# The landing buffer of a mixture-of-experts stage: its loads issued from GpSimd's own queue instead of SyncE's

## The chip, the cores and the metric

One core of a Trainium2 chip runs the whole program. The metric is the device time of one execution in microseconds. The program is one launch that computes two transformer blocks; the change touches one stage of the first of them, the experts.

## The reference, cut to what matters

Both blocks work on 512 tokens of width 1024, in float32. The stage in question is the feed-forward part of the first block: each token is sent to 4 of 32 experts, and the rows of an expert are gathered and padded to whole blocks.

```python
logits = (xt @ w_router) + b_router
top_v, top_e = lax.top_k(logits, 4)            # 512 tokens x 4 of 32 experts
top_w = softmax(top_v)
# rows sorted by expert, padded per expert to whole blocks; then for each block of rows, expert e:
g = xb @ w_gate[e] + b_gate[e]                 # 1024 x 1024, the first product
u = xb @ w_up[e] + b_up[e]                     # 1024 x 1024, the second
g = minimum(g, 7); u = clip(u, -7, 7)
act = (u + 1) * (g * sigmoid(1.702 * g))
y = act @ w_down[e] + b_down[e]                # 1024 x 1024, the third
```

## The kernel before, in words

The kernel pads an expert's rows to blocks of 64 (the reference to 128; the outcome is the same). An expert's weights are three matrices of 4 MB, each cut into 4 units of 1 MB that lie in memory as 128 rows of 8 KB: units 0 to 3 are the gate matrix, 4 to 7 the up matrix, 8 to 11 the down matrix. In on-chip memory there is one place for each of the 12 units, `wt[:, 0..11]`, and a landing buffer `land[:, 0..3]` for the 4 units of the third product (down) alone. So at most 16 units are held at once, while the stage moves 31 x 12 of them (expert 0's are loaded by the stage before).

TensorE (`pe`) walks over the blocks. For block i it runs gate(i), two transposes, up(i), and then down(i - 1): the third product is one block late. Each unit is 8 matmuls of 512 columns (two halves of the array work side by side). After a unit it raises `s_mm[u]`. Before a unit it waits: for units 0 to 7 on `s_w[u]` (the load has landed), for units 8 to 11 on `s_cp[u - 8]` (GpSimd has copied it out of the landing buffer).

SyncE (`sp`) loops over the experts e = 1 to 31 and issues all loads of an expert in a fixed order: gate units 0 to 3, the biases (`biases(e)`, line 1111), up units 4 to 7 (all through `unit(u)`, line 1122), and then the four landing units (line 1133). `done` is the number of the last block of expert e - 1. Each gate or up unit waits until TensorE has used that place for the last block of the expert before; each landing unit waits until GpSimd has emptied that row, `s_cp[u]` at least e.

GpSimd (`pool`) loops over the same experts: for each of the 4 landing rows it waits for the load, and for TensorE to have finished with the place in `wt` (`s_mm[8 + u]`), and then copies the row over (line 1150). That wait ends while TensorE runs the third product of the last block of expert e - 1, which comes behind gate and up of expert e's first block.

ScalarE issues the loads of the blocks' rows (`load`, line 1231, two of 128 KB a block) and the stores of the results (`store`, line 1235, two of 128 KB a block) in a hardware queue of its own, q10. SyncE's loads go in the hardware queue q1. What GpSimd issues goes in the software queue q0. All queues are served by the same 16 DMA engines.

Of the kernel before, what the change touches and what calls it, by code (L numbers as in the profile page):

```python
# [33 lines left out]
NE, TOPK = 32, 4  # L34
# [16 lines left out]
def take(nc, name):  # L51

    TAKEN.append(nc.alloc_semaphore(name))
    return TAKEN[-1]
# [9 lines left out]
def build(nc, A, K, out, dram):  # L64

    with ExitStack() as ctx:
# [11 lines left out]
        with ExitStack() as early:  # L78
            wt = sb("wt", [P, NUNIT, 2, D], c=early)
            s_w = [nc.alloc_semaphore(f"e_w{u}") for u in range(NUNIT)]  # L80
            with ExitStack() as first:
                flat = wt[:, :, :, :].rearrange("p u k n -> p (u k n)")
                qkv = flat[:, 0:12 * D].rearrange("p (b a t w) -> p b a t w", b=2, a=3, t=NT)
                ring = flat[:, 12 * D:].rearrange("p (n k w) -> p n k w", n=3, k=KD)
                gB = flat[:, 0:KD * T].rearrange("p (f t) -> p f t", f=KD)
                mT = flat[:, 6 * D:6 * D + KD * T].rearrange("p (f t) -> p f t", f=KD)
                yT = sb("yT", [P, 2, NT, T], c=first)
                hT = sb("hT", [P, KD, T], c=first)
                s_wb = [nc.alloc_semaphore(f"g_wb{u}") for u in range(2)]
                first_mix(nc, A, K, dram, ident, tri, mod, x, ps, yT, hT, qkv, ring, mT, gB, s_wb)  # L90
                end_stage(nc)
                first_merge(nc, A, K, dram, ident, tri, mod, x, ps, yT, hT, ring, mT, gB, blocks, pos, w4, wt, s_w, s_wb)
                end_stage(nc)
            experts(nc, A, K, dram, ident, ps, blocks, wt, s_w)
            end_stage(nc)
# [979 lines left out]
def experts(nc, A, K, dram, ident, ps, blocks, wt, s_w):  # L1075

    with ExitStack() as ctx:
        def sb(name, shape, dt=F32):
            return ctx.enter_context(nc.sbuf_tensor("e_" + name, shape, dt))

        def sem(name):
            return take(nc, "e_" + name)
# [10 lines left out]
        land = sb("land", [P, 4, 2, D])  # L1093
# [2 lines left out]
        TAKEN.extend(s_w)  # L1096
        s_mm = [sem(f"mm{u}") for u in range(NUNIT)]
        s_cp = [sem(f"cp{u}") for u in range(4)]
        s_raw, s_shuf, s_xg = (sem(n) for n in ("raw", "shuf", "xg"))
        s_xt, s_xT, s_g, s_sig, s_act = (sem(n) for n in ("xt", "xT", "g", "sig", "act"))  # L1100
        s_at, s_aT, s_y, s_out, s_dve, s_go = (sem(n) for n in ("at", "aTs", "y", "out", "dve", "go"))
# [4 lines left out]
        with nc.Block() as block:  # L1106
            @block.sync
            def _(sp):
                def biases(e):
                    for q in range(4):  # L1110
                        sp.dma_start(raw[32 * q:32 * q + 1, :, :].rearrange("p a n -> p (a n)"),
                                     A["b_exp"][bass.ds(e, 1)].rearrange("e q n -> e (q n)")[:, q * 3 * W:(q + 1) * 3 * W]
                                     ).then_inc(s_raw, 16)

                sp.wait_ge(s_shuf, 1)
                biases(0)
                with sp.Fori(1, NE) as e:
                    done = sp.value_load(blocks[0:1, bass.ds(e + FIRST, 1)], min_val=0, max_val=NBLK)

                    def unit(u):  # L1120
                        sp.wait_ge(s_mm[u], done * 2 + 2)
                        sp.dma_start(wt[:, u].rearrange("p k n -> p (k n)"),
                                     A["w_exp"][bass.ds(e, 1)].rearrange("e u p n -> p (e u) n")[:, u, :]).then_inc(s_w[u], 16)

                    for u in range(4):
                        unit(u)
                    sp.wait_ge(s_shuf, done + 1)
                    biases(e)
                    for u in range(4, 8):
                        unit(u)  # L1130
                    for u in range(4):
                        sp.wait_ge(s_cp[u], e)
                        sp.dma_start(land[:, u].rearrange("p k n -> p (k n)"),
                                     A["w_exp"][bass.ds(e, 1)].rearrange("e u p n -> p (e u) n")[:, 8 + u, :]).then_inc(s_w[8 + u], 16)
                for u in range(NUNIT):
                    sp.wait_ge(s_w[u], 16 * NE)
                sp.wait_ge(s_raw, 64 * NE)

            @block.gpsimd
            def _(pool):  # L1140
                for u in range(4):
                    pool.wait_ge(s_w[8 + u], 16)
                    pool.sem_inc(s_cp[u], 1)
                with pool.Fori(1, NE) as e:
                    done = pool.value_load(blocks[0:1, bass.ds(e + FIRST, 1)], min_val=0, max_val=NBLK)
                    for u in range(4):
                        pool.wait_ge(s_w[8 + u], e * 16 + 16)
                        pool.wait_ge(s_mm[8 + u], done * 2 + 2)
                        pool.sem_inc(s_go, 1)
                        nc.gpsimd.tensor_copy(wt[:, 8 + u], land[:, u]).then_inc(s_cp[u], 1)  # L1150
                for u in range(4):
                    pool.wait_ge(s_cp[u], NE)

# [1661 lines left out]
```

## Time and profile before

| | us |
|---|---|
| median of 3 runs | 3922.02 |
| lowest, highest run | 3916.95, 3926.28 |
| the profiled execution's own time | 3920.97 |
| its span | 3919.2 |

The page of the profile has a first part with the busy time of each engine, a second with the span in 40 slices of 98 us (busy tenths of each engine, the granted clock of TensorE, the share in which the DMA engines were busy, and GB/s), a list of the queues, and a list of the costliest groups of instructions. The stage of the experts is some 1255 us of the span, from about 799 to about 2054 us, slices 9 to 21. Timelines give for one engine the start, the time taken, the instruction, and in brackets how long the engine had been idle just before and what ended that.

### The profile page before, as it was taken

The page shows a single profiled execution, that of the slowest core. Times are in us where ns is not written, and L with a number is a line of the kernel's source. Part 1 is how long each engine was busy: PE and PEld are TensorE (multiplying, and loading weights), DVE is VectorE, ACT ScalarE, POOL GpSimd, SP SyncE. Part 2 cuts the span into 40 slices and gives each one's busy share as a digit, 9 for nine tenths or more (in the row PEclk, how much of TensorE's full clock was granted, in tenths as well). Part 3 has the DMA queues.
Part 4 walks back from the last instruction along what each step waited for, and adds up shares of the span by engine and source line. Part 5 has one row for each costly group of instructions (what it writes and reads, how often), then busy time and mean ns, then how long its engine had stood idle before and what let it go on. Part 6 is the DMA issues. An engine that isn't in the chain of part 4 may idle for free. (4 is left out here: it accounts for less than half of the span.)

```text
span 3919.2 us, 37507 instructions
## 1 busy us (share of the span) xinstructions
PE 3376.9 (86%) x11902; PEld 1491.6 (38%) x11903; DVE 1928.6 (49%) x3951; ACT 688.9 (18%) x1609; POOL 964.2 (25%) x829
## 2 busy tenths in 40 slices
PE   7997999788889987999887987898878888788887
PEld 3345454422223322333224456544333333333332
DVE  5834323622333322333225226486666766766776
ACT  1011121000000000000002125422222222222212
POOL 1000000112221222012122013134443444444443
PEclk8998999789999999999998998999998999999998
DMA  9834434469999999197976201179999999999998
GB/s 330 285 124 166 152 122 157 187 240 411 370 375 353 363 407 374 62 380 270 397 290 242 81 6 44 44 291 378 421 421 399 417 417 412 421 404 421 415 422 341
DMA packets 194149, 1157.36 MB, mean 295 GB/s; under 512 B 25659, under 2 KB 27995, under 8 KB 74356
## 3 DMA queue, kind: packets, MB, share of 16 engines
q1 hardware_dynamic: 97140, 565.17, 37.3%
q0 software_dynamic: 80576, 564.05, 35.2%
q10 hardware_dynamic: 16320, 26.75, 2.2%
q8 instruction: 57, 0.93, 0.1%
q14 instruction: 56, 0.46, 0.0%
HBM read 1128.96 MB, written 48.68 MB: 300 GB/s over the span
## 5 line engine op out<-in xcount | busy, mean ns | idle before, releaser
L1170 PE MATMUL ps<-wt,e_xT 128*64 128x512 f32 x3200 | 743.4, 609 | 114.2 <-DMA wt<-in_w_exp 113.0
L2628 DVE SCALAR_TENSOR_TENSOR mod<-uv,mix 128x1024 f32<-128x1024 f32 x512 | 626.9, 1225 | 352.4 <-DMA uv<-in_peer_uv,q_picks 347.7
L2312 POOL DMA_INDIRECT uv<-in_peer_uv,q_picks x512 | 575.4, 1124 | 773.4 <-PE ps L2403 702.7
L2403 PE MATMUL ps<-uv,q_dg 128*128 128x512 f32 x1024 | 519.9, 664 | 134.4 <-ACT q_dg L2480 129.9
L2403 PE MATMUL ps<-uv,tri 128*128 128x512 f32 x1024 | 472.2, 615 | 75.9 <-ACT tri L2480 75.9
L1150 POOL COPY wt<-e_land 128x2048 f32<-128x2048 f32 x124 | 248.0, 2030 | 1004.3 <-PE ps L1170 951.8
L1170 PEld LDWEIGHTS ps<-wt,e_xT 128*64 128x64 f32 x3200 | 219.7, 139 | 596.2 <-issue 380.8
L2403 PEld LDWEIGHTS ps<-uv,q_dg 128*128 128x128 f32 x1024 | 213.7, 214 | 431.7 <-issue 431.7
L1170 PE MATMUL ps<-wt,e_aT 128*64 128x512 f32 x1600 | 354.2, 595 | 2.8 <-ACT e_aT L1223 2.8
L2403 PEld LDWEIGHTS ps<-uv,tri 128*128 128x128 f32 x1024 | 197.8, 197 | 345.6 <-issue 345.6
L472 PE MATMUL ps<-hT,wt 128*128 128x512 f32 x640 | 285.1, 602 | 1.5 <-DVE wt L799 1.5
L1289 DVE TENSOR_TENSOR e_ut<-ps,e_bias 128x512 f32<-128x512 f32 x50 | 34.6, 692 | 400.6 <-PE ps L1170 400.6
L1223 ACT COPY e_aT<-ps 128x512 f32<-128x512 f32 x50 | 29.3, 585 | 1095.0 <-PE ps L1158 1072.5
L1170 PEld LDWEIGHTS ps<-wt,e_aT 128*64 128x64 f32 x1600 | 115.3, 138 | 232.8 <-issue 232.8
L2474 ACT ACTIVATE q_ap<-q_ap 128x4 f32<-128x4 f32 (+1 forms) x131 | 26.9, 205 | 893.6 <-DVE mod L2628 893.6
L472 PEld LDWEIGHTS ps<-hT,wt 128*128 128x128 f32 x640 | 120.8, 192 | 151.0 <-issue 145.1
L684 DVE SCALAR_TENSOR_TENSOR x<-mod,small,x 128x512 f32<-128x512 f32 x168 | 129.3, 769 | 32.5 <-DMA mod<-in_w_ada_units 20.9
L1306 DVE TENSOR_TENSOR e_yb<-ps,e_bias 128x512 f32<-128x512 f32 x50 | 34.6, 692 | 171.9 <-PE ps L1170 171.9
L472 PE MATMUL ps<-wt,hT 128*128 128x512 f32 x256 | 116.5, 611 | 0.7 <-ACT hT L574 0.7
L1278 DVE LOAD_MASK_SELECT e_bias<-e_raw x50 | 0.7, 14 | 211.0 <-DMA e_raw<-in_b_exp 163.8
L2358 PE MATMUL ps<-q_hT,q_wq 128*128 128x512 f32 x224 | 98.4, 592 | 0.0
L405 POOL COPY mod<-hT 128x1024 f32<-128x1024 f32 x4 | 8.2, 2063 | 365.5 <-PE ps L472 365.5
(458 smaller groups left out, 3508.3 us busy)
## 6 DMA issues: line engine op xcount, KB each, us to landing
wt<-in_w_exp SPq DMA_DIRECT2D x260, 1024.0 KB, 20.0
e_land<-in_w_exp SPq DMA_DIRECT2D x124, 1024.0 KB, 24.2
wt<-in_w_in_units SPq DMA_DIRECT2D x15, 2048.0 KB, 11.2
mod<-in_w_mod_units SPq DMA_DIRECT2D x48, 512.0 KB
scratch_xs<-const_zeros SPq DMA_DIRECT2D x8, 2080.0 KB
mod<-in_w_ada_units SPq DMA_DIRECT2D x32, 512.0 KB
p_ring<-in_w_in SPq DMA_DIRECT2D x7, 2048.0 KB, 10.6
e_xg<-scratch_xs ACTq DMA_DIRECT2D x104, 128.0 KB
```

The costliest lines, as they stand in the source:

```text
L472: last = nc.tensor.matmul(ps[:, j, :], lhs, rhs, start=(k == 0), stop=(k == kt - 1))
L684: last = dve.scalar_tensor_tensor(at, quarter[:, q, kk, :], cs[:, v, k:k + 1], at, ALU.mult, ALU.add)
L1150: nc.gpsimd.tensor_copy(wt[:, 8 + u], land[:, u]).then_inc(s_cp[u], 1)
L1170: ins = nc.tensor.matmul(ps[64 * h:64 * h + 64, at, :], lhs[:, k % 4, 64 * (k // 4):64 * (k // 4) + 64], wt[:, u, a, h * W:(h + 1) * W], s ...
L1223: nc.scalar.copy(dst, ps[:, at, :].rearrange("p (k q) -> p k q", k=4)).then_inc(kept, 1)
L1289: link(dve.tensor_tensor(ut[:, :], ps[:, U, :], bias[:, 1, :], ALU.add))
L1306: dve.tensor_tensor(yb[:, :], ps[:, Y, :], bias[:, 3, :], ALU.add).then_inc(s_y, 1)
L2312: pool.indirect_dma_start(out=uv[:, slot(n), :, :].rearrange("p a d -> p (a d)"), out_offset=None, in_=A["peer_uv"], in_offset=bass.Indire ...
L2358: last = nc.tensor.matmul(ps[:, 6 + c, :], wq[:, h % 2, k, c * NK:(c + 1) * NK], hT[:, k, :], start=(k == 0), stop=(k == KD - 1))
L2403: last = nc.tensor.matmul(acc(t)[:, c, :], dg(n), uv[:, slot(n), 1, c * W:(c + 1) * W], start=fresh, stop=closing)
L2474: act.activation(at, at, ACT.Gelu).then_inc(s_ge, 1)
L2628: dve.scalar_tensor_tensor(junk[:, n % 2, :], uv[:, slot(n), 0, :], 1.0, mix[:, tile_of(k), :], ALU.mult, ALU.mult, accum_out=ap[:, k % 2, ...
```

## The change

The four landing loads leave SyncE's loop and are issued by GpSimd. Expert 1's are issued at the start of the stage, when expert 0's third-product units have landed in `wt`; expert e + 1's unit u is issued right after the copy of expert e's unit u has ended, before the next copy. A new semaphore for each row, `s_ld[u]`, counts their landing. The loop over experts on GpSimd is split so that the last expert has no load behind it.

```diff
+        s_ld = [sem(f"ld{u}") for u in range(4)]
@@ sync
                     for u in range(4, 8):
                         unit(u)
-                    for u in range(4):
-                        sp.wait_ge(s_cp[u], e)
-                        sp.dma_start(land[:, u].rearrange("p k n -> p (k n)"),
-                                     A["w_exp"][bass.ds(e, 1)].rearrange("e u p n -> p (e u) n")[:, 8 + u, :]).then_inc(s_w[8 + u], 16)
                 for u in range(NUNIT):
-                    sp.wait_ge(s_w[u], 16 * NE)
+                    sp.wait_ge(s_w[u], 16 * NE if u < 8 else 16)
@@ gpsimd
                 for u in range(4):
                     pool.wait_ge(s_w[8 + u], 16)
                     pool.sem_inc(s_cp[u], 1)
-                with pool.Fori(1, NE) as e:
+                    pool.dma_start(land[:, u].rearrange("p k n -> p (k n)"), A["w_exp"][1, 8 + u]).then_inc(s_ld[u], 16)
+
+                def unload(e, following):
                     done = pool.value_load(blocks[0:1, bass.ds(e + FIRST, 1)], min_val=0, max_val=NBLK)
                     for u in range(4):
-                        pool.wait_ge(s_w[8 + u], e * 16 + 16)
+                        pool.wait_ge(s_ld[u], e * 16)
                         pool.wait_ge(s_mm[8 + u], done * 2 + 2)
                         pool.sem_inc(s_go, 1)
                         nc.gpsimd.tensor_copy(wt[:, 8 + u], land[:, u]).then_inc(s_cp[u], 1)
+                        if following:
+                            pool.wait_ge(s_cp[u], e + 1)
+                            pool.dma_start(land[:, u].rearrange("p k n -> p (k n)"),
+                                           A["w_exp"][bass.ds(e + 1, 1)].rearrange("e u p n -> p (e u) n")[:, 8 + u, :]).then_inc(s_ld[u], 16)
+
+                with pool.Fori(1, NE - 1) as e:
+                    unload(e, True)
+                unload(NE - 1, False)
```

## Rows read from the trace of the kernel before

**Rows 1.** The page, 40 slices: share of DMA in tenths; slices 9 to 21 are the stage.

```profile
DMA  9834434469999999197976201179999999999998
```

**Rows 2.** Waits, 780 to 2160 us: who waited for whom, us in total, times, longest.

```profile
SPq L1122 <- PE ps L1170: 657.5, 185, 112.0
...
PE ps L1170 <- DMA wt<-in_w_exp: 113.0, 106, 3.6
```

**Rows 3.** Timeline of GpSimd: copies out of the landing buffer, and three DMA issues.

```profile
994.34 6.06 POOL L1150 COPY wt<-e_land 128x2048 f32<-128x2048 f32 x3 [25.00 <-PE ps L1170]
1027.48 8.09 POOL L1150 COPY wt<-e_land 128x2048 f32<-128x2048 f32 x4 [25.02 <-PE ps L1170]
1071.03 8.09 POOL L1150 COPY wt<-e_land 128x2048 f32<-128x2048 f32 x4 [35.46 <-PE ps L1170]
1099.15 1.93 POOL L1150 COPY wt<-e_land 128x2048 f32<-128x2048 f32 x1 [20.03 <-PE ps L1170]
...
1559.75 8.08 POOL L1150 COPY wt<-e_land 128x2048 f32<-128x2048 f32 x4 [24.83 <-PE ps L1170]
1690.39 8.09 POOL L1150 COPY wt<-e_land 128x2048 f32<-128x2048 f32 x4 [122.56 <-PE ps L1170]
...
2068.91 2.81 POOL L1414 DMA_DIRECT2D p_cw<-in_conv_w  x3
```

**Rows 4.** Timeline of SyncE's queue from the load of expert 7's gate units on.

```profile
1034.35 5.48 SPq L1122 DMA_DIRECT2D wt<-in_w_exp  x4
...
1048.05 1.88 SPq L1133 DMA_DIRECT2D e_land<-in_w_exp  x4
...
1106.02 5.48 SPq L1122 DMA_DIRECT2D wt<-in_w_exp  x4
```

**Rows 5.** Timeline of TensorE over experts 6 (two blocks), 7 (one) and 8.

```profile
1047.17 7.04 PE L1170 MATMUL ps<-wt,e_aT 128*64 128x512 f32 x32
...
1068.94 7.04 PE L1170 MATMUL ps<-wt,e_aT 128*64 128x512 f32 x32
...
1079.80 1.94 PE L1170 MATMUL ps<-wt,e_xT 128*64 128x512 f32 x8 [0.39 <-DMA wt<-in_w_exp]
...
1095.29 1.94 PE L1170 MATMUL ps<-wt,e_xT 128*64 128x512 f32 x8 [0.97 <-DMA wt<-in_w_exp]
```

**Rows 6.** Windows: us, PE, PEld, DVE, ACT, POOL busy (x), PEclk, DMA share, GB/s.

```profile
1101.00:1107.00 6.00, 6.00 (x32) 2.00 (x30) 1.80 (x3) 0.00 (x0) 5.87 (x4) 1.00 0.30 107
1565.00:1655.00 90.00, 90.00 (x432) 31.61 (x430) 28.37 (x52) 6.81 (x12) 2.73 (x2) 1.00 0.10 25
940.00:1020.00 80.00, 61.27 (x258) 18.35 (x254) 19.69 (x30) 5.11 (x9) 15.90 (x8) 0.94 1.02 410
```

**Rows 7.** DMA queues, 2066 to 2072 us: packets, MB, share of 16 engines' time.

```profile
DMA packets 871, 2.45 MB, mean 409 GB/s; under 512 B 62, under 2 KB 62, under 8 KB 871
...
q0 software_dynamic: 435, 1.58, 65.8%
q1 hardware_dynamic: 436, 0.87, 37.6%
```

**Rows 8.** DMA queues, 97 to 102 us, and below them the page's for the whole span.

```profile
DMA packets 446, 1.64 MB, mean 329 GB/s; under 512 B 45, under 2 KB 45, under 8 KB 446
...
q0 software_dynamic: 257, 0.93, 61.0%
...
q0 software_dynamic: 80576, 564.05, 35.2%
```

**Rows 9.** The start of the stage: ScalarE's queue and TensorE.

```profile
795.51 1.22 ACTq L1231 DMA_DIRECT2D e_xg<-scratch_xs  x2
799.04 1.11 PE L1158 MATMUL ps<-ident,e_xg 128*128 128x128 f32 x4 [37.61 <-DMA e_xg<-scratch_xs]
```

**Rows 10.** Timeline of VectorE: one operation without and with GpSimd's copies beside it.

```profile
856.94 0.69 DVE L1293 TENSOR_TENSOR e_ut<-e_ut,e_sg 128x512 f32<-128x512 f32 x1
...
900.49 2.17 DVE L1293 TENSOR_TENSOR e_ut<-e_ut,e_sg 128x512 f32<-128x512 f32 x1
```

## The prediction, made before the changed kernel was run

> **What bounds the kernel now.** I read the 40 slices first [rows 1]. In slices 9 to 21, the experts, the DMA engines are busy at nine tenths or more except in three kinds of place, and so I went to the waits [rows 2]: SyncE's queue waits 657 us for TensorE to free a place, and TensorE waits for loads again and again, 113 us as the matmuls see it, in pieces of under 4 us. Neither wait alone says what the stage costs; it is a pipeline with 16 places that is bound by transfers in some stretches and by TensorE in others.
>
> The copies out of the landing buffer show which is which [rows 3]. Copy k starts when TensorE reaches the third product of the block before expert k, so the distance from copy k to copy k+1 is the time of expert k. There are 31 starts. The distances take these values: 33.1 us (994.34 to 1027.48), 43.55 us (to 1071.03), about 28.1 us (to 1099.15; 27.0 to 28.3 in all ten that follow an expert of several blocks), and 65.3 or 130.64 us (1559.75 to 1690.39). TensorE needs 21.77 us for a block (down to down, 1047.17 to 1068.94 [rows 5]), so 43.55 is two blocks at TensorE's own pace, 65.3 three, 130.64 six. The others are single blocks that took 6 to 11 us longer than TensorE needs. The counts come out as: expert 1 three blocks, 21 six, 26 three, experts 6, 8, 10, 11, 13, 15, 23, 25 and 29 two, the other 20 one: 50 blocks, 1089 us at TensorE's pace, against some 1255 us.
>
> Single experts in a row are bound by transfers: the DMA share is 1.02 over 940 to 1020 us, at 410 GB/s [rows 6], and 12 units take 33.1 us, 2.76 us a unit with the blocks' rows in between. At 410 GB/s a unit of 1.05 MB alone is 2.55 us: one slot, below. Experts of many blocks leave the engines idle: share 0.10 in 1565 to 1655 us, 0.30 in 1101 to 1107 us [rows 6].
>
> What limits a 28.1 us expert is the order in the queue. SyncE restarts at R = 1034.35 us with expert 7's gate units, after the gate product of expert 6's last block [rows 4]. From there the queue carries gate 7, up 7, land 7, gate 8, up 8, land 8. TensorE can go on past up 8 only when the 20th unit from R is there; its last matmuls wait for it until 1095.29 [rows 5]. Only then follow down, the next gate product and the next restart at 1106.02. So the measure is: how many slots stand ahead of the last up unit of the two-block expert that closes a group? For a group of m experts (the single ones, and the one that closes it) it is now 8m + 4(m-1) = 12m - 4.
>
> **What the change does to that count.** SyncE's queue keeps its order but loses the landing units: 8m slots. The landing units of expert k+1 start when expert k's are copied, in a second queue that shares the engines.
>
> What share does it get? The direct evidence is a stretch where both queues had work throughout: in 2066 to 2072 us q0 moved 435 packets and q1 moved 436 [rows 7], one for one. In 97 to 102 us GpSimd's queue had 61% of the time [rows 8]. Units of 8 KB rows in either queue then mean half each. Over the span q0 moved 564 MB in 80576 packets [rows 8], 7 KB each, so its rows of 8 KB stay whole, too.
>
> Now the pair 7, 8. Copy 6 starts at 1027.48; a copy is 1.93, an issue on GpSimd 0.94 (2.81 for three [rows 3]), and about 1.3 us pass before data move (an estimate: 1106.02 issue, share back by 1107 [rows 4, 6]). Data of land 7 flow from 1031.7, SyncE's from 1035.6: p = 1.5 of its 4 units are ahead in otherwise idle time. The other 2.5 share. Land 8 starts at 1071.03 + 4.2 = 1075.2. By then, before the change, some 14 of the 20 slots are moved (the 15th is used at 1079.80, after some 3 us of landing, the 20th at 1095.29 [rows 5]). After it 2.5 of these 14 are land 7, and 4.5 of SyncE's 16 are still to come. Against these, at one for one, all 4 units of land 8 go through as well. So 16 + 2.5 + 4 = 22.5 slots instead of 20: **+2.5 slots, 6.4 us**. In words: a load that stood last in the one queue now takes every second packet from loads that TensorE is about to need, and is itself not needed until 20 us later. The same count for a longer group gives 12m - 1.5 against 12m - 4, again +2.5.
>
> Groups that follow a two-block expert, from the list above: 7-8, 9-10, 12-13, 14-15, 16-21, 24-25, 30-31. **Seven times 6.4 = 44.8 us.**
>
> Groups behind three or six blocks have p = 4: the landing units are all in before R, which is the real gain of the change. Groups 2-6 and 27-29: 12m - 4 on both sides, 0 (expert 2 gains some 5 us, expert 3 gives them back). Group 22-23 is so short that land 23 gets only 2 units in before SyncE's last two are done: 18 slots against 20, **-5.1 us**.
>
> Experts 10 and 11, two blocks each in a row, run at TensorE's pace with idle DMA time now and go on so: 0.
>
> *GpSimd's own chain.* Four copies take 8.09 us; with an issue and a wait for the copy's own end (some 0.3 us) behind each, 4 x (1.93 + 0.3 + 0.94) = 12.7 us. An issue three times as long, 2.82, would make it 20.2. The copy started 2.1 us after down began (1068.94 to 1071.03), and the next down, 21.8 us or more after it, first needs unit 8, copied first: unit 11 is needed 25 us after the copies' start. 0 on the path; cover 5 us at worst. Nothing else is queued on GpSimd in this stage.
>
> *The start.* Expert 1's landing units are issued when GpSimd enters the stage, at about the time of the first load of rows, 795.51, for which TensorE waits until 799.04 [rows 9]. Its packets alternate with 8 KB ones: 8 of its packets on each engine, 0.3 us more each (8 KB at 410/16 GB/s), less the microsecond that GpSimd needs to issue: **+2 us**, bounds 0 and 3. By the time that expert 1's first units are awaited, 25 us later, the four are through.
>
> *SyncE.* Four issues and waits fewer for each expert; it waits for TensorE in any case [rows 2]: 0. At the stage's end it waits for the same loads as before: 0.
>
> Sum: 3920.97 (the profiled execution; median of the runs 3922.02) + 44.8 - 5.1 + 2 = **3963 us**. Its own bounds: the slot may cost up to 3.1 us where rows are loaded and stored in it (1079.80 to 1095.29, five units), seven times 2.5 x 0.55 = 10 more; and two queues at once may move less than one. With both at work the rows show 409 GB/s [rows 7] and 329 [rows 8], against 410 for one; 409 I take, since those transfers, like these, ask for more than the engines move throughout. At 329 in the 16 us or so that four landing units share per expert it would be 3 us for each of some 25 experts, 80 us; I give that end little weight, and 20 us of it to the range. 3940 to 3995.
>
> **Rivals.** (1) The new queue is served less than it asks: faster. If q0 gets nothing while q1 has work, the landing units only fill the idle time: the seven groups then have 12m - 5.5 slots, -3.8 us each, -27; the three groups behind three or six blocks gain up to the whole excess over TensorE's pace at their first expert and don't give it back, -27. 3920.97 - 54 = 3867. The deciding point is the share: with a third of the packets, land 8 moves 2.25 units against 4.5, +0.75 slots seven times is +13, against some -13 elsewhere, so below a third it is faster. For it: q0's software descriptors may come late. Against: the one-for-one count and the 61%. 16%, at 3867 to 3914.
>
> (2) No difference. The bytes and the 16 engines are the same, single experts stay at 33.1 us, and the added slots are balanced by the prefetch behind the long experts: 3914 to 3929. 12%. The Trainium skill ("Trainium Kernel Development and Optimization", Key Constraints) has a rule for this: transfers issued from SyncE, ScalarE and GpSimd run on the same 16 engines and interleave, so that a second issuer saves only issue time; by it the time would be 3921. The trace agrees that they interleave, and it is the interleaving that I count a price for.
>
> (3) Far worse: GpSimd's chain reaches the third product late, or the two queues run at the 329 end. VectorE and GpSimd do hold each other up: a product of VectorE that takes 0.69 us takes 2.17 beside GpSimd's copies [rows 10]. The chain has 12 us to spare in all, so an issue would have to lose 3 us each time before TensorE waits; each microsecond beyond costs one on each of 31 experts. 4%, some 4010.
>
> **Chances.** My forecast 68%, rival 1 16%, rival 2 12%, rival 3 4%. Runs of this kernel tell 0.2% (8 us) from no change. Slower by more than that: 0.72; within it: 0.12; faster: 0.16. The range reaches down into rival 1 only as far as needed: 3903 to 3995; my own case alone is 3940 to 3995.
>
> **What would show it.** In the profile after: the copies' distances of single experts behind two-block ones, 28.1 now, should be 33 to 35; expert 2 and 27 should be down at 22 to 23, expert 3 and 28 up at about 38; 33.1 should stay in rows of single experts. The waits of TensorE on `wt` should grow by some 40 us. DMA idle time should stand behind the last up unit. The queue list should show q0 with some 130 MB more and q1 as much less. I'd be wrong if the distances of 28.1 shrink towards 22 to 25 (the share is less than a third), or if the single rows leave 33.1 by more than 1 us either way (two queues together move more or less than one).

## The result, and the profile after

The changed kernel takes 3982.72 us (median; 3974.5 to 3986.55) against 3922.28 for the one before. The ratio is 1.0152, with a 95% interval of 1.0132 to 1.0173: 60 us slower. The forecast was 3963, within 3903 to 3995.

The profiled execution took 3981.15 us, with a span of 3979.5. First the queue list and two groups of the page, for what moved where (queues: packets, MB, share of 16 engines; groups: busy us, mean ns of one, idle time just before and what ended it):

```profile
q0 software_dynamic: 98432, 694.08, 43.1%
q1 hardware_dynamic: 79284, 435.14, 28.5%
...
L1178 PE MATMUL ps<-wt,e_xT 128*64 128x512 f32 x3200 | 783.0, 640 | 130.5 <-DMA wt<-in_w_exp 129.7
...
L1150 POOL COPY wt<-e_land 128x2048 f32<-128x2048 f32 x124 | 236.9, 1912 | 922.4 <-PE ps L1178 922.4
```

GpSimd's queue carries 130 MB more, 124 units of 1.05 MB. TensorE's wait for `wt` went from 113.0 us [rows 2] to 129.7, only 17 us. The same group of the page before:

```profile
L1170 PE MATMUL ps<-wt,e_xT 128*64 128x512 f32 x3200 | 743.4, 609 | 114.2 <-DMA wt<-in_w_exp 113.0
```

The matmuls of gate and up are 31 ns longer on average, and 40 us more in sum. Both will be needed.

The timeline of GpSimd answers [rows 3] (only the first copies of each expert are shown, and the issues of one):

```profile
966.43 1.92 POOL L1150 COPY wt<-e_land 128x2048 f32<-128x2048 f32 x1 [25.71 <-PE ps L1178]
...
999.67 1.92 POOL L1150 COPY wt<-e_land 128x2048 f32<-128x2048 f32 x1 [20.92 <-PE ps L1178]
...
1034.54 1.89 POOL L1150 COPY wt<-e_land 128x2048 f32<-128x2048 f32 x1 [22.55 <-PE ps L1178]
...
1078.87 1.92 POOL L1150 COPY wt<-e_land 128x2048 f32<-128x2048 f32 x1 [32.03 <-PE ps L1178]
1081.46 0.53 POOL L1153 DMA_DIRECT2D e_land<-in_w_exp  x1 [0.66 <-POOL wt L1150]
1081.98 1.90 POOL L1150 COPY wt<-e_land 128x2048 f32<-128x2048 f32 x1
...
1113.87 1.93 POOL L1150 COPY wt<-e_land 128x2048 f32<-128x2048 f32 x1 [22.68 <-PE ps L1178]
...
1740.01 1.92 POOL L1150 COPY wt<-e_land 128x2048 f32<-128x2048 f32 x1 [118.32 <-PE ps L1178]
...
1761.94 1.92 POOL L1150 COPY wt<-e_land 128x2048 f32<-128x2048 f32 x1 [9.62 <-PE ps L1178]
```

Expert 6 (two blocks) takes 44.3 us from copy to copy, expert 7 takes 35.0 where it was 28.1, expert 22, behind the one of six blocks, 21.9 where it was 28.3. Here are all 31 copies, added up by the groups of the prediction:

| part | forecast, us | measured, us |
|---|---|---|
| start, up to copy 1 (835.07 before, 839.42 after) | +2 | +4.4 |
| the seven groups behind two-block experts | +44.8 | +55.9 (7.7, 7.5, 8.5, 9.7, 8.0, 7.6, 7.1) |
| group 22-23 | -5.1 | -6.1 |
| groups 2-6 and 27-29 | 0 | +3.3 and +1.1 |
| experts 1, 11 and 26 | 0 | +0.7 |
| sum, up to copy 31 (2031.01 before, 2090.28 after) | +41.7 | +59.3 |

Of the signs that the prediction named, the single experts behind two-block ones take 35.0 to 36.4 us, at and above the end of its 33 to 35. Two signs stood against it: the waits, 17 us and not 40, and single experts in a row, which were to stay at 33.1 us within 1 us. Experts 17 to 20 take 32.7, 34.0, 30.8 and 35.2 us (32.9 to 33.1 before). Their sum, 132.8 us against 132.2, has hardly moved, so two queues don't move less together; but the time shifts from one expert of a group to the next, and this sign was too sharp for that.

### The profile page after: what moved, and what is told of

The parts are those of the page before. It is cut to its first block and busy times, and to the rows that moved or that the text cites. A ratio compares the mean times of both kernels' runs of the same rounds, so it can differ in the third digit from the quotient of the medians.

```text
span 3979.5 us, 37527 instructions
## 1 busy us (share of the span) xinstructions
PE 3402.7 (86%) x11902; PEld 1496.6 (38%) x11903; DVE 1985.3 (50%) x3951; ACT 689.0 (17%) x1609; POOL 1023.2 (26%) x953
## 5 line engine op out<-in xcount | busy, mean ns | idle before, releaser
L1178 PE MATMUL ps<-wt,e_xT 128*64 128x512 f32 x3200 | 783.0, 640 | 130.5 <-DMA wt<-in_w_exp 129.7
L2411 PE MATMUL ps<-uv,q_dg 128*128 128x512 f32 x1024 | 507.0, 651 | 137.6 <-ACT q_dg L2488 137.6
L1150 POOL COPY wt<-e_land 128x2048 f32<-128x2048 f32 x124 | 236.9, 1912 | 922.4 <-PE ps L1178 922.4
L1178 PEld LDWEIGHTS ps<-wt,e_xT 128*64 128x64 f32 x3200 | 231.3, 145 | 635.2 <-issue 427.6
L1231 ACT COPY e_aT<-ps 128x512 f32<-128x512 f32 x50 | 29.3, 586 | 1159.8 <-PE ps L1166 1128.1
L1459 PE MATMUL ps<-p_ring,p_hT 128*128 128x512 f32 (+1 forms) x256 | 97.4, 542 | 0.0
```

Of the source, the lines that this page charges most:

```text
L1178: ins = nc.tensor.matmul(ps[64 * h:64 * h + 64, at, :], lhs[:, k % 4, 64 * (k // 4):64 * (k // 4) + 64], wt[:, u, a, h * W:(h + 1) * W], s ...
L1459: last = nc.tensor.matmul(ps[:, m % NBANK, 0:rhs.shape[1]], lhs, rhs, start=(k == 0), stop=(k == KD - 1))
L2411: last = nc.tensor.matmul(acc(t)[:, c, :], dg(n), uv[:, slot(n), 1, c * W:(c + 1) * W], start=fresh, stop=closing)
```

## Experiments: is it the place in the order, or the software queue?

**Theory A** is the prediction's: the engines take a packet from each queue in turn, so landing units go ahead of gate and up units that TensorE needs sooner. **Theory B**: GpSimd's software queue is itself the price, through late descriptors, a longer chain on GpSimd or a lower rate.

**The same queue, issued later.** GpSimd issues the four units after expert e+1's last up unit has landed.

```diff
-                        if following:
-                            pool.wait_ge(s_cp[u], e + 1)
-                            pool.dma_start(land[:, u], ...)          # expert e + 1
+                    if following:
+                        for u in range(4):
+                            pool.wait_ge(s_cp[u], e + 1)
+                        pool.wait_ge(s_w[7], e * 16 + 32)
+                        for u in range(4):
+                            pool.dma_start(land[:, u], ...)          # expert e + 1
```

> The landing units stay in GpSimd's software queue, but GpSimd issues expert e+1's four only when expert e+1's last up unit (unit 7) has landed. Theory A (the cost comes from landing units that take every second packet from gate and up units): in a group of two the count ahead of the last up unit is 20 slots again, so the seven groups lose nothing; only the start (+4 us) stays: 3926 us, 3915 to 3935, single experts behind two-block ones back at about 28 us. Theory B (the software queue itself is what costs: late descriptors, GpSimd's longer chain, a lower rate): the queue and its number of transfers are as in the changed kernel, so most of the +60 us stays: 3965 to 3985.

Measured: 3931.33 us, ratio 1.0027 (1.0017 to 1.0036). 51 of the 60 us are gone with all 124 transfers still in the software queue. GpSimd's timeline shows the issues behind the up units' landing:

```profile
1028.04 2.28 POOL L1157 DMA_DIRECT2D e_land<-in_w_exp  x4 [4.97 <-DMA wt<-in_w_exp]
1033.30 1.90 POOL L1150 COPY wt<-e_land 128x2048 f32<-128x2048 f32 x1 [2.98 <-DMA e_land<-in_w_exp]
...
1076.56 1.90 POOL L1150 COPY wt<-e_land 128x2048 f32<-128x2048 f32 x1 [8.77 <-DMA e_land<-in_w_exp]
...
1104.71 1.90 POOL L1150 COPY wt<-e_land 128x2048 f32<-128x2048 f32 x1 [2.87 <-DMA e_land<-in_w_exp]
```

Expert 7 is back at 28.2 us (1076.56 to 1104.71). The copies now wait for their loads and not for TensorE, so they are a weaker measure here; TensorE's own third products, at 1072.74 and 1100.71, give 28.0 us. The seven groups are back within 0.4 us in sum. Of the 8.4 us by which copy 31 is late, 3.6 are at the start (copy 1 at 838.7), 2.2 in group 27-29, 1.1 in expert 1 and 0.8 in group 2-6; why these lose I didn't trace.

**One hardware queue, but early.** The kernel before, SyncE's order gate, land, up instead of gate, up, land; nothing on GpSimd's queue.

```diff
-                    for u in range(4, 8):
-                        unit(u)
                     for u in range(4):
                         sp.wait_ge(s_cp[u], e)
                         sp.dma_start(land[:, u], ...)
+                    for u in range(4, 8):
+                        unit(u)
```

> The kernel before, all loads in SyncE's hardware queue, but its order is gate, land, up instead of gate, up, land. Theory A: the landing units of the closing expert now stand wholly ahead of its up units: 12m slots instead of 12m - 4, 4 slots or 10.2 us in each of ten groups: about 4020 us, 3995 to 4035, with no software queue at all; single experts in a row stay at 33.1 us. Theory B: nothing goes through GpSimd's queue, so the time is that of the kernel before, 3915 to 3930.

Measured: 4046.25 us, ratio 1.0313 (1.0296 to 1.033). Theory B would have it at 3922. GpSimd's and TensorE's timelines:

```profile
843.37 8.07 POOL L1150 COPY wt<-e_land 128x2048 f32<-128x2048 f32 x4 [59.14 <-PE ps L1170]
...
1045.39 8.09 POOL L1150 COPY wt<-e_land 128x2048 f32<-128x2048 f32 x4 [24.98 <-PE ps L1170]
1093.83 8.08 POOL L1150 COPY wt<-e_land 128x2048 f32<-128x2048 f32 x4 [40.36 <-PE ps L1170]
1127.17 8.09 POOL L1150 COPY wt<-e_land 128x2048 f32<-128x2048 f32 x4 [25.25 <-PE ps L1170]
1175.58 8.09 POOL L1150 COPY wt<-e_land 128x2048 f32<-128x2048 f32 x4 [40.32 <-PE ps L1170]
```

```profile
1115.71 9.54 PE L1170 MATMUL ps<-wt,e_xT 128*64 128x512 f32 x32 [9.04 <-DMA wt<-in_w_exp]
```

Experts 7 and 8 take 1175.58 - 1093.83 = 81.75 us, 10.1 more than the 71.67 of before. Four slots of 2.55 us are 10.2. The nine groups that the copies show whole cost 10.0 to 11.4 us each, 93.3 in sum (the last, 30-31, is cut off at copy 31). The total is 26 us above what I expected, and it is not in the groups. Copy 1 comes 8.3 us later (843.37, not 835.07): TensorE waits 8.05 us for expert 1's up units, which now stand behind expert 1's landing units. Experts 1, 11 and 26, which have several blocks and belong to no group, cost 4.6, 4.4 and 5.0 us: from SyncE's restart to the last up unit of the expert behind stand 12 slots where 8 stood, and TensorE now waits for these units, too (3.7 us in expert 12's first up product). My expectation had put nothing there.

The agreement of 10.1 with 10.2 is in part luck. Before expert 8's first up product TensorE waits 9.04 us, and then the product takes 9.54 us and not 7.09. So some 2.4 of the 10.1 us are a slow product, and the four slots alone cost less than 10.2.

**Half of the units.** Units 0 and 1 early on GpSimd's queue, 2 and 3 in SyncE's queue behind the up units.

```diff
+                    for u in (2, 3):                                  # sync, behind the up units
+                        sp.wait_ge(s_cp[u], e)
+                        sp.dma_start(land[:, u], ...).then_inc(s_ld[u], 16)
@@ gpsimd, expert 1
-                    pool.dma_start(land[:, u], ...)
+                    if u < 2:
+                        pool.dma_start(land[:, u], ...)
@@ gpsimd, expert e + 1
-                        if following:
+                        if following and u < 2:
```

> Two of the four landing units (0 and 1) go early in GpSimd's queue, two (2 and 3) stay in SyncE's queue behind the up units. Theory A: for a group of two 16 + 2 units of SyncE's and 0.5 + 2 of GpSimd's, 20.5 slots: +0.5 slot, 1.3 us, seven times, and 1 to 2 us at the start: 3922 + 9 + 2 = 3932 us, 3922 to 3942. Theory B (cost in proportion to what goes through the software queue): half of +60: 3950, 3945 to 3958.

Measured: 3939.61 us, ratio 1.0043 (1.0029 to 1.0058): +17 us, nearer to A's +10 than to B's +30, and within A's bounds. Experts 7 and 8 take 29.3 and 43.5 us, +1.2 where the count says +1.3; the seven groups cost 11.1 us in sum where it says 9, and copy 1 is 4.2 us late where I expected 1 to 2. The cost isn't in proportion: half of the units cost a third.

**Smaller packets in one of the queues.** The changed kernel, each landing unit loaded by two transfers with rows of 4 KB.

```diff
-                        pool.wait_ge(s_ld[u], e * 16)
+                        pool.wait_ge(s_ld[u], e * 32)
...
-                            pool.dma_start(land[:, u].rearrange("p k n -> p (k n)"), ...[:, 8 + u, :]).then_inc(s_ld[u], 16)
+                            for k in range(2):
+                                pool.dma_start(land[:, u, k], ...[:, 8 + u, k * D:(k + 1) * D]).then_inc(s_ld[u], 16)
```

> As the changed kernel, but each landing unit is loaded by two transfers with rows of 4 KB in place of one with rows of 8 KB, so that GpSimd's queue has packets half as large. Theory A in its sharp form (the engines take one packet from each queue in turn): q0 gets a third of the bytes while both have work instead of half, land 8 gets 2.25 units in against SyncE's last 4.5, 20.75 slots instead of 22.5: the seven groups lose 2 us each instead of 8, and the groups behind long experts gain some 3 to 5 each: 3920 to 3945 us. If the share goes by bytes or by time, whatever the packets' size, or if the software queue itself costs (eight issues in place of four, GpSimd's chain 14.6 us): 3975 to 3995.

Measured: 3944.89 us, ratio 1.0056 (1.004 to 1.0073). The same bytes, in the same queue, behind the same copies, with twice the issues, and 38 of the 60 us are gone. It lies at the upper end of what I expected, and by the copies the parts differ: the seven groups still lose 29.8 us in sum where the count says 14, groups 22-23 and 27-29 gain 4.5 each, as forecast, and group 2-6 loses 1.0. The queue lists of both kernels for 1085 to 1095 us, while both have expert 8's units under way. Changed kernel:

```profile
DMA packets 693, 4.21 MB, mean 421 GB/s; under 512 B 82, under 2 KB 82, under 8 KB 214
...
q0 software_dynamic: 269, 2.06, 49.5%
q1 hardware_dynamic: 265, 1.88, 45.2%
```

With packets of 4 KB:

```profile
q1 hardware_dynamic: 310, 2.21, 54.6%
q0 software_dynamic: 358, 1.28, 34.0%
```

269 packets against 265, half the bytes each; with small packets 358 against 310 and 37% of the bytes. The share goes by packets, near one for one; by bytes it would have been half, and by time as well. It also answers what two queues with rows of 8 KB can move: 421 GB/s here, and 406 over 940 to 1020 us, where the kernel before moved 410 [rows 6].

**The start.** Expert 1's landing units are issued only when TensorE has turned the rows of its second block.

```diff
                     pool.sem_inc(s_cp[u], 1)
+                pool.wait_ge(s_xt, 2)
+                for u in range(4):
                     pool.dma_start(land[:, u], ...)                  # expert 1
```

> The changed kernel, but expert 1's four landing units are issued only when TensorE has turned the second block's rows (the first rows are then in). Theory A: the start is a price of its own, 4.2 us late in the changed kernel because the first rows shared the engines with these units; it comes back, 3978.5 us, 3974 to 3982, first copy at about 835 us; the rest of the stage is as in the changed kernel. Rival: the first rows are late for another reason, and the time stays at 3982 to 3984.

Measured: 3984.03 us, ratio 1.0162 (1.0148 to 1.0176): no gain over the changed kernel. TensorE's timeline, with the issue on GpSimd's between:

```profile
796.61 1.12 PE L1168 MATMUL ps<-ident,e_xg 128*128 128x128 f32 x4 [37.52 <-DMA e_xg<-scratch_xs]
...
808.95 2.20 POOL L1143 DMA_DIRECT2D e_land<-in_w_exp  x4 [24.38 <-PE ps L1168]
...
831.78 3.68 PE L1180 MATMUL ps<-wt,e_xT 128*64 128x512 f32 x8 [3.90 <-DMA wt<-in_w_exp]
```

The first rows are in at 796.61 and no longer at 803.27: that the landing units delayed them is right. But those units now run beside expert 1's up units, TensorE waits for these, and the first copy comes at 844.7 instead of 839.4. What the start gave back was lost 30 us later, by the same mechanism. It is these rows that decide it: the intervals of the two ratios overlap, and the totals alone wouldn't exclude a gain of 4 us. The 4 us aren't a price of their own that can be taken off.

**Early only where the engines idle.** GpSimd reads from the list of blocks whether expert e has two or more. If so, it issues each unit right behind its copy; else it waits for expert e+1's last up unit.

```diff
+                    behind = pool.value_load(blocks[0:1, bass.ds(e + FIRST + 1, 1)], min_val=0, max_val=NBLK)
+                    with pool.If(done + 1 < behind):
+                        for u in range(4):
+                            copy(e, u, done)
+                            load(e, u)
+                    with pool.If(behind < done + 2):
+                        for u in range(4):
+                            copy(e, u, done)
+                        pool.wait_ge(s_w[7], e * 16 + 32)
+                        for u in range(4):
+                            load(e, u)
```

> GpSimd issues expert e+1's landing unit right behind the copy only where expert e has two or more blocks (the engines are idle then); else it issues them once expert e+1's last up unit has landed. Theory A by the count: the seven groups behind two blocks have 16 + 2.5 = 18.5 slots in place of 20, -3.8 us each, the three groups behind three or six blocks 12m - 8 in place of 12m - 4, -10 us or down to TensorE's pace, together -27; with +4 at the start: 3922 - 54 + 4 = 3872 us, 3865 to 3895. Theory B (the software queue itself costs) or C (a second queue can bring nothing, since the bytes and engines are the same): 3922 to 3935.

Measured: 3899.8 us, ratio 0.9944 (0.9929 to 0.9959), faster than both kernels: by 22 us than the one before (by 20 than its runs made beside these, median 3920.04), by 83 than the changed one. So a second queue can bring something, and theory C falls; but it is less than half of the 50 us I expected. TensorE's timeline over expert 7's first products and expert 8's says why:

```profile
1055.80 1.94 PE L1194 MATMUL ps<-wt,e_xT 128*64 128x512 f32 x8 [1.06 <-DMA wt<-in_w_exp]
...
1061.56 1.94 PE L1194 MATMUL ps<-wt,e_xT 128*64 128x512 f32 x8 [1.52 <-DMA wt<-in_w_exp]
...
1086.81 1.94 PE L1194 MATMUL ps<-wt,e_xT 128*64 128x512 f32 x8 [0.33 <-DMA wt<-in_w_exp]
```

My count looked only at the last up unit of a group. That one is hardly waited for now (0.33 us). But TensorE waits at expert 7's own up units, which the remaining 2.5 landing units delay: the bound moved one expert forward. And expert 8's landing units, issued behind up 8, come in late for their copies, so expert 9's start late in turn and less of them fits into the idle time. Experts 7 and 8 take 24.4 and 46.4 us, 0.8 less than before and not 3.8. Over the stage the seven groups gain 10.5 us where I counted 27, and the three behind long experts 15.1, where I also counted 27. I followed the reason in the rows of experts 7 and 8 alone.

The same with the later start:

> The same with expert 1's landing units issued after the second block's rows are turned. Theory A: 4 us less than the one before: 3868 us, 3861 to 3891. Theory C: 3918 to 3931.

Measured: 3904.6 us, ratio 0.9962 (0.9949 to 0.9976). Not 4 us less, as far as runs of this spread can tell; copy 1 comes at 844.8 us and not at 837.8, the same flaw as in the later start above.

## Why the prediction came out as it did, step by step

**What bounds the kernel: right, within limits.** The reading as groups in which slots stand ahead of the last up unit carried over to three variants: +10.1 us for four slots in one queue (in part by luck, see there), +1.2 for half a slot, 28 us with the old order in the new queue. It fell short where another expert's units became the ones waited for: in the version that is early only where the engines idle it promised 27 us in the seven groups, and 10.5 came; with rows of 4 KB they lost twice what it says.

**The share: right.** One packet for one was read off a stretch of another stage [rows 7]; in the stage itself it is 269 against 265, and the experiment with 4 KB rows shows that packets are what is counted. Rival 1 (served less than it asks) needed a share below a third. (Its second -27 was too large by its own words: the first experts behind the three long ones lay 6.1, 6.5 and 5.5 us above TensorE's pace, 18 in sum.) The rule of the Trainium skill that I weighed in rival 2 ("Trainium Kernel Development and Optimization", Key Constraints: all queues run on the same engines, so a second one saves only issue time) has two parts. The trace agrees that the queues interleave on the same engines, 269 packets against 265. The "only" fell in this kernel on both sides: the second queue cost 60 us where it was early, and the conditional version gained 22.

**The seven groups: right in kind, 20% short.** 7.1 to 9.7 us each, 55.9 in sum, not 44.8. TensorE after the change, over expert 8's first up product, to be held against [rows 5]:

```profile
1095.31 3.68 PE L1178 MATMUL ps<-wt,e_xT 128*64 128x512 f32 x8 [3.60 <-DMA wt<-in_w_exp]
1101.21 3.41 PE L1178 MATMUL ps<-wt,e_xT 128*64 128x512 f32 x8 [2.23 <-DMA wt<-in_w_exp]
1106.60 5.35 PE L1178 MATMUL ps<-wt,e_xT 128*64 128x512 f32 x16 [1.98 <-DMA wt<-in_w_exp]
1111.78 7.04 PE L1178 MATMUL ps<-wt,e_aT 128*64 128x512 f32 x32
```

The restart of SyncE's queue that belongs to it, and the third product of before that stands against the one at 1111.78:

```profile
1041.41 5.48 SPq L1123 DMA_DIRECT2D wt<-in_w_exp  x4
```

```profile
1097.06 7.04 PE L1170 MATMUL ps<-wt,e_aT 128*64 128x512 f32 x32
```

A unit that took 1.94 us takes 3.68. The windows of both kernels, first the changed one (columns as in [rows 6], the clock third from the end):

```profile
1091.00:1112.00 21.00, 13.20 (x41) 3.69 (x41) 2.14 (x3) 1.70 (x3) 0.18 (x1) 0.67 0.75 293
```

```profile
1075.00:1097.00 22.00, 16.83 (x78) 5.15 (x76) 4.31 (x8) 1.70 (x3) 4.12 (x3) 1.00 1.01 406
```

The granted clock is 0.67 in this stretch where it was 1.00: it falls while TensorE stands idle for 3.60 us (0.85 on average over 1091.00 to 1095.31), and the unit behind that wait runs at 0.50, 1.2 instead of 2.4 GHz. In the same product of the kernel before the waits were 0.55 to 1.52 us, and the clock stayed at 1.00. The first two units have time for that, since the next one isn't there anyway. The last two don't (0.60 over 1107.50 to 1111.80): 5.35 us, not 1.94 + 1.76 = 3.70, so 1.65 us late. From the restart to the next down it was 1097.06 - 1034.35 = 62.7 us and is 1111.78 - 1041.41 = 70.4: +7.7, of which 6.0 are the slots (forecast 6.4) and 1.65 the clock. The same reading of all seven groups (from the last unit that was waited for to the third product, less 1.77 us a unit) gives 1.4 to 2.9 us each, 13.0 in sum; in the kernel before it gives 0.0 in every group. That leaves 42.9 us for the slots, where the count said 44.8. So the term that was missing from my sum, which had nothing for it, is that a wait of this length has a tail: the work right behind it runs at half the clock. It shows in the one-queue experiment, too: behind the wait of 9.04 us for the up units the product took 9.54 us for 7.09. There the tail didn't come on top of 10.2 us, though; it was within them. I took no run in which the clock alone was changed, so the split is read from rows, not isolated.

It also corrects what I wanted to see as evidence: TensorE's waits grew by 17 us, not by 40. The other 40 us stand as busy time, in slower matmuls. Waits and busy time together are 56, near the 55 that the stage lost between its copies.

**Behind the long experts: right.** Expert 22 at 21.9 us, expert 2 at 23.7 and expert 27 at 21.8, then 38.0 and 38.9 for experts 3 and 28, near the forecast (22 to 23, and about 38); -6.1 for group 22-23. Groups 2-6 and 27-29 lost 3.3 and 1.1 in place of 0. In group 2-6 the clock's tail behind the last wait is 1.7 of the 3.3 us; in group 27-29 there is none, and its 1.1 stay open.

**GpSimd's chain: right, by luck so near.** Four copies took 12.3 us with their issues (forecast 12.7), because two misses cancel: an issue took 0.53 us and not 0.94, and the wait for the copy's end 0.66 and not 0.3. Nothing waited for them. Rival 3 had no part.

**The start: right in kind, a third of the size.** Copy 1 is 4.4 us late for a forecast of 2, beyond my bound of 3, and even that hides a part. ScalarE issued the load of the first rows at 793.61 us in the changed kernel, 1.9 us earlier than in the kernel before (795.51); from issue to use they took 9.66 us and not 3.53 [rows 9]:

```profile
793.61 1.22 ACTq L1239 DMA_DIRECT2D e_xg<-scratch_xs  x2
```

```profile
803.27 1.12 PE L1166 MATMUL ps<-ident,e_xg 128*128 128x128 f32 x4 [43.80 <-DMA e_xg<-scratch_xs]
```

So the landing units cost the first rows 6.1 us. The other traces agree: 3.3 to 3.6 us where no landing unit is issued beside the rows, 7.9 to 8.9 where some are. And as the experiment shows, it isn't separable.

**The DMA share: as forecast.** Behind the last up unit the engines now stand idle, 0.04 of the time in 1110 to 1118 us, since what could have filled that time is already loaded. The bytes moved ahead in the order didn't vanish; the idle time went behind them:

```profile
1110.00:1118.00 8.00, 8.00 (x38) 2.72 (x36) 3.98 (x4) 0.00 (x0) 3.47 (x3) 0.93 0.04 6
```

## What to carry to other kernels

A queue's order is also its priority. A load that is needed last and stands last in a full queue delays only what stands behind it; in a queue of its own it gets about as many packets as the other, and what it takes it takes from the load that is needed next. Count the transfers that stand ahead of the one the engine waits for, before and after, for the expert before as well, since the wait can move there; expect the work behind a longer wait to be slower, too; and let a second queue run early only where the first one is empty. The share between queues goes by packets, so the size of a row sets it.

## What the runs showed of the hardware that I had not expected

The two queues' share is nearly exactly by packet: 269 to 265 with rows of 8 KB in both, and 358 to 310, 37% of the bytes, when one has rows of 4 KB. Halving the rows of the less urgent queue alone was worth 38 us.

Two queues at once moved 421 GB/s in 1085 to 1095 us. Over 940 to 1020 us they moved 406 GB/s, where the kernel before moved 410 [rows 6]: the mixture is hardly slower.

VectorE's time depends on where GpSimd's copies fall, though nobody waits for it here. Its copy of the biases, a median of 0.49 us before, has a median of 2.53:

```profile
L1305 DVE COPY e_bias<-e_bias x50: 419/2528/2536, 825.3 to 2096.1; 128x512 f32<-128x512 f32 x50
```

Its busy time in the whole execution rose from 1928.6 to 1985.3 us. That isn't a price of the new queue as such: with the issues held back behind the last up unit, and with rows of 4 KB, the median is 0.43 us, and with half of the units in each queue 4.36. I didn't isolate the cause.
